# Other orders of rounding, turns, sums and loads at ten places of a two-block fp32 kernel

## The reference

```python
# block 1, layer 0: the input is a norm of x, scaled and shifted by rows of c @ w_mod + b_mod
u = h @ w_in                         # q, k, v, gates, z for 4 heads of 256; the pool's input
y_m = head_norm(mlstm(q, k, v) + mlstm_reversed(q, k, v)) * sigmoid(...) * silu(...)
y_p = ((window_mean(u) - u) @ pool_w) * scale * silu(...)     # windows 2, 4, 8, 16
x = x + gate * norm(concat(y_m, y_p) @ w_out)
# block 1, layer 1: 16 heads of 64 over 4 key heads, rotary positions, window of 128 and context, a sink
x = x + gate * norm((attention(q, k, v) * silu(z)) @ w_out)
# block 2
x = x + concat(gla(...), diff_attention(...)) @ w_out         # 4 heads each
x = x + (silu(conv(h @ w_up_a)) * conv(h @ w_up_b)) @ w_down  # 2816 wide
x = x + sigmoid(h @ w_gate) * (p @ w_proj)                    # the "ple" stage
out = norm(x) * norm_final
```

## Time and profile before

| | us |
|---|---|
| median of 3 runs | 3405.12 (3401.29 to 3410.22) |
| the profiled execution's own time | 3408.22 |
| its span in the trace | 3406.4 |
| PE busy | 3296.8 (17536 products) |
| DVE busy | 1765.3 |
| ACT busy | 1510.5 |
| POOL busy | 110.6 |
| mean granted clock of PE | 0.988 |

### The profile page before, as it was taken

How to read it: one execution, slowest core, us unless ns; L and a number is a source line. 1 busy time by engine, 2 the same in 40 slices (tenths; PEclk the granted TensorE clock), 3 DMA queues, 4 the chain that set the end, 5 groups by cost and what they waited for, 6 DMA issues and landing times. The chain is left out here.

```text
span 3406.4 us, 42773 instructions
## 1 busy us (share of the span) xinstructions
PE 3296.8 (97%) x17536; PEld 2664.9 (78%) x17536; DVE 1765.3 (52%) x2736; ACT 1510.5 (44%) x2411; POOL 110.6 (3%) x240
## 2 busy tenths in 40 slices
PE   7999999999999999999999999998999999999997
PEld 5988889797777777887887777775778888878775
DVE  6544444444344467532886644359556544444544
ACT  5343434434224345215786534228435444433445
POOL 2000000000000000001000000000000000000000
PEclk8999999999999999999999999999999999999999
DMA  5202011111333556122301711010331111134553
GB/s 203 70 1 81 29 54 55 53 56 38 141 134 105 190 207 247 56 50 71 91 2 38 195 53 50 26 54 1 130 118 50 50 50 43 44 130 161 179 185 130
DMA packets 187442, 308.38 MB, mean 91 GB/s; under 512 B 28507, under 2 KB 122560, under 8 KB 187120
## 3 DMA queue, kind: packets, MB, share of 16 engines
q1 hardware_dynamic: 165392, 227.60, 20.8%
q0 software_dynamic: 20784, 77.98, 6.5%
q10 hardware_dynamic: 1072, 0.07, 0.0%
HBM read 269.87 MB, written 35.75 MB: 90 GB/s over the span
## 5 line engine op out<-in xcount | busy, mean ns | idle before, releaser
L412 DVE TENSOR_TENSOR W_rounded<-W,W_rounded 128x2048 fp32r<-128x2048 f32 (+1 forms) x172 | 348.9, 2029 | 469.5 <-ACT W_rounded L403 465.7
L403 ACT ACTIVATE W_rounded<-W 128x2048 fp32r<-128x2048 f32 (+1 forms) x172 | 292.5, 1701 | 398.2 <-DMA W<-in_w_down 97.0
L3587 PE MATMUL G<-HT_rounded,W_rounded 128*128 128x512 f32 x1584 | 452.8, 393 | 0.0
L3587 PEld LDWEIGHTS G<-HT_rounded,W_rounded 128*128 128x128 f32 x1584 | 298.3, 188 | 68.4
L2551 PE MATMUL G<-W_rounded,r_y_rounded 128*128 128x512 f32 x960 | 229.7, 400 | 6.1 <-DVE r_y_rounded L2657 4.7
L2551 PE MATMUL G<-W_rounded,x_hi 128*128 128x512 f32 x704 | 222.1, 397 | 3.6 <-DVE act_turned_rounded L2657 3.3
L2551 PEld LDWEIGHTS G<-W_rounded,r_y_rounded 128*128 128x128 f32 x960 | 181.0, 190 | 51.7 <-DVE W_rounded L412 5.7
L2204 PE MATMUL G<-HT_rounded,W_rounded 128*128 128x512 f32 (+1 forms) x768 | 210.1, 358 | 3.7 <-DVE W_rounded L412 3.7
L1151 PE MATMUL G<-W_rounded,HT_rounded 128*128 128x512 f32 x640 | 213.6, 415 | 0.0
L3587 PE MATMUL G<-HT_lo_ffn,W_rounded 128*128 128x512 f32 x528 | 208.5, 395 | 0.0
L1195 PE MATMUL G<-HT_rounded,W_rounded 128*128 128x512 f32 (+1 forms) x768 | 205.7, 354 | 1.0 <-PEq L652 1.0
(11 more groups left out here) (479 smaller groups left out, 6468.9 us busy)
## 6 DMA issues: line engine op xcount, KB each, us to landing
W<-in_w_down SPq DMA_DIRECT2D x33, 1024.0 KB, 4.9
W<-in_ab_w_out SPq DMA_DIRECT2D x32, 1024.0 KB, 5.5
W<-in_w_up SPq DMA_DIRECT2D x44, 512.0 KB, 5.0
W<-in_ab_w_in SPq DMA_DIRECT2D x20, 1024.0 KB, 8.7
W<-in_w_mod SPq DMA_DIRECT2D x8, 2048.0 KB, 8.1
x_rows<-r_xt POOLq DMA_DIRECT2D x32, 512.0 KB, 5.5
W<-in_c_w_out SPq DMA_DIRECT2D x24, 512.0 KB, 7.0
r_xt<-x_rows POOLq DMA_DIRECT2D x24, 512.0 KB, 5.1
```

The source lines that it names most:

```text
L403: ins = a.activation(self.half(key, True)[:, at], self.half(key, False, False)[:, at], ACT.Copy)
L412: ins = v.tensor_tensor(self.half(key, False)[:, at], self.half(key, False, False)[:, at], self.half(key, True)[:, at].bitcast(F32), ALU.s ...
L3587: ins = pe.matmul(bank(("up", j, half))[:, rc * 512:rc * 512 + 512], w[a][:, k, c], x[b][:, 2 * rc:2 * rc + 2, :], start=(k == 0 and a == ...
```

## The change

Ten places get another order; no weight product is added or removed.

1. Start: one 1 MB load moves from SP's queue to POOL's; DVE copies the fourth part's rows ahead of two low parts, and rounds the first weight half after them.
2. Heads: the rounding of the next head's first half is done in four pieces at steps 11 to 14 instead of one at step 10.
3. The four late turns are made in two pairs, after the first and second row chunk of the first gemm, and ACT's copies with them; the same at the seam to the pool.
4. Pool: `wlo(1)` comes before `prev.done(v)` and the windows.
5. Attention: the last block's rounding is split into head pairs 0 to 6 and pair 7.
6. `rows_part`, gated: `before_split(s)` row sums come before the rounding, the others after it. Not gated: all row sums come before the following stage's rounding.
7. `rows_part`, `tail`: the up projection's first piece is rounded at the end of the step instead of before the row work.
8. Differential attention: the small loads move from SP to POOL, the scores of steps 2 to 15 alternate between the halves of `S`, GLA's turns go to the upper half of `TP` with one buffer instead of two, and one instruction gets another form.
9. ple: the gates of the last two rows follow their Relu; the last projection goes into a free bank of G.
10. ple: the last row's product, sum, scaling and store are made in halves, and stored by SP.

```diff
@@ phase_start
-            for j in range(4):
+            for j in (0, 2, 3):
                 load_mod(sp, j, 0)
...
-            for j in range(4):
+            load_mod(g, 0, 1)
+            for half in range(2):
+                load_mod(g, 1, half)
+            for j in (2, 3):
                 load_mod(g, j, 1)
...
             mod_rows(2)
+            mod_rows(3)
             low(2)
-            mod_rows(3)
             mod_cols(2)
-            low(3)
             mod_cols(3)
             shifts(4)
             value(4)
             value(6)
+            for k in range(3, KT):
+                low(k)
             K.split_lo(v, ("qk", 0, 0))
-            for k in range(4, KT):
-                low(k)
@@ mlstm_part: tensor, (scalar alike), vector
-                if ct == 0 and h >= 1:
-                    for n in late:
-                        turn_y(pe, h - 1, n)
+                    if h >= 1 and ct == 0 and rc < 2:
+                        for n in late[2 * rc:2 * rc + 2]:
+                            turn_y(pe, h - 1, n)
...
-                if s == 10:
-                    K.split_lo(v, ("qk", h + 1, 0) if h + 1 < H else ("p", 0, 0))
+                if 11 <= s < 15:
+                    K.split_lo(v, ("qk", h + 1, 0) if h + 1 < H else ("p", 0, 0), s - 11, 4)
@@ attend_part
+    rounded = [(bi, 0, 8) for bi in range(XT - 1)] + [(XT - 1, 0, 7), (XT - 1, 7, 8)]
@@ pool_part: tensor, vector
+                if (gi, ct) == (0, 0) and rc_ < 2:
+                    prev.turn(pe, rc_)
...
                 if gi == ct == 0:
+                    wlo(1)
                     prev.done(v)
...
-                if gi == ct == 0:
-                    wlo(1)
@@ rows_part: scalar and vector
+    def before_split(s):
+        rows = ended(s)
+        if per >= 8:
+            return 1
+        return len(groups[s // per]) if s < len(steps) else len(rows)
...
-            for r in rows[:1] if per >= 8 else rows:
+            for r in rows[:before_split(s)]:
                 act_y(r)
...
-            if s == len(steps) and following:
+            if not gated:
+                for r in ended(s):
+                    add(r)
+            if s == len(steps) + int(not gated) and following:
                 K.split_lo(v, following[1])
...
-            for r in ended(s)[:1] if per >= 8 else ended(s):
-                add(r)
+            if gated:
+                for r in ended(s)[:before_split(s)]:
+                    add(r)
...
-                if tail is not None:
-                    tail[2](v, 0)
...
                     B.vec_turned(v, r, TR, *turned(r))
+            if s == len(steps) - 1 and tail is not None:
+                tail[2](v, 0)
@@ diff_part
-    gla_steps = [1, 3, 5, 7, 9, 11, 13, 14]
+    gla_steps = [1, 3, 5, 7, 9, 11, 13, 15]
...
+    def s_at(j):
+        return 512 * ((j + 1) % 2) if 2 <= j < 16 else 0
...
-            if j >= 1:
+            if j == 2:
+                mix.taken(pe)
+            elif 3 <= j < 16:
+                pe.wait_ge(s_nm, 2 * j - 2)
+            elif j >= 1:
                 pe.wait_ge(s_nm, 2 * j)
...
-            if r >= 2:
-                pe.wait_ge(s_gl, r - 1)
+            if r >= 1:
+                pe.wait_ge(s_gl, r)
...
-            if j == 16:
+            if j == 18:
                 pe.wait_ge(s_gl, XT)
...
-            ch.link(v.tensor_scalar(cw[:, j:j + 1], sm[:, j, 0:1], rc[:, j, 1:2], lam[:, 3:4], ALU.mult, ALU.mult))
+            ch.link(v.scalar_tensor_tensor(out=cw[:, j:j + 1], in0=sm[:, j, 0:1], scalar=lam[:, 3:4], in1=rc[:, j, 1:2],
+                                           op0=ALU.mult, op1=ALU.mult))
@@ ple_part
+    def product(r):
+        return G[:, (r + 1) % 3, :] if r == XT - 1 else PP[:, :]
...
-            if r:
+            if r == XT - 1:
+                pe.wait_ge(s_gread, r - 1)
+            elif r:
                 pe.wait_ge(s_pp, r)
...
+                    if s == len(steps):
+                        gate(r)
...
+                halves = [slice(0, 512), slice(512, D)] if r == XT - 1 else [slice(0, D)]
...
-            for r in due(s, 2):
+            for r in [] if s == len(steps) else [XT - 3, XT - 2] if s == len(steps) + 2 else due(s, 2):
```

More of the change, by code:

```diff
@@ L1269, in evacuate @@
                 K.free_bank(a.activation(raw[:, ct % 2, p0:p0 + n], G[:, K.par(key), 0:n], ACT.Copy), key)
+                if h >= 1 and ct == 0 and rc < 2:
+                    for q in late[2 * rc:2 * rc + 2]:
+                        copy_turned_y(a, h - 1, q)
         def take_v(h, r):
@@ L2602, in scalar @@
                     a.activation(y_part(s, 1), y_part(s, 0, False), ACT.Copy).then_inc(s_yhi, 1)
-            if s == len(steps) - 1:
-                if following:
-                    K.split_hi(a, following[0])
-                if tail is not None:
-                    tail[1](a, 0)
-            for r in rows[1:] if per >= 8 else []:
+            if s == len(steps) - 1 and following:
+                K.split_hi(a, following[0])
+            for r in rows[before_split(s):]:
                 act_y(r)
@@ L2658, in vector @@
                         .then_inc(s_ylo, 1)
-            if s == len(steps) - 1:
-                if following:
-                    K.split_lo(v, following[0])
-                if tail is not None:
-                    tail[2](v, 0)
-            for r in ended(s)[1:] if per >= 8 else []:
+            if s == len(steps) - 1 and following:
+                K.split_lo(v, following[0])
+            for r in ended(s)[before_split(s):] if gated else []:
                 add(r)
@@ L3250, in sync @@
     def sync(sp):
[L3251 to L3256 removed]
+        pass
     def turn_diff(pe, bi):
@@ L3826, in scalar, with gate @@
         ch = Chain(a, K.a_chain, K.an)
+        def gate(r):
+            e = ge[:, r % 3, :]
+            a.wait_ge(s_gread, r + 1)
+            ch.link(a.activation(e, e, ACT.Exp, bias=K.cut[:, :], scale=-1.0))
+            ch.link(a.activation(e, e, ACT.Ln, bias=K.one[:, :]))
+            a.activation(e, e, ACT.Exp, scale=-1.0).then_inc(s_sg, 1)
         for s in range(2, len(steps) + 5):
```

108 lines of the change are left out of this document (56 added, 52 removed).

## The result

The changed kernel takes 3369.7 us (median of 4 runs, 3365.7 to 3374.2) against 3406.9 us (median of 4, 3401.3 to 3410.2): 37.1 us less, a ratio of 0.9883 with a 95% interval of 0.9864 to 0.9903. The forecast was 39.1 us less and 3366.

A forecast was written before the change was run, and what follows sets the result against it. PE was taken to bound the kernel, busy 3296.8 of 3406.4 us, leaving 109.6 us idle and half-clock stretches to win. Ten terms summed to 39.1 us off the 3405.1 median: 3366, range 3352 to 3388.

The forecast's parts named there:

- three signs of being wrong: PE idle time falling under 20 us, new waits over 1 us where a rounding moved, PE busy time moving over 10.
- Start: At the start, DVE's earlier copy removes a 1.63 us wait and the moved load gives 0.7: −2.3 us (0 to −5).
- the rule weighed in the forecast: Transfers from any engine share 16 DMA engines; the start's moved load would give 0 instead of 0.7, forecast 3366.7.
- Heads: In four heads, quartered rounding removes four 1.59 us waits, −6.4; late turns in pairs give 0.8 each, −3.2.
- Pool: At the pool, DVE's earlier rounding removes PE's 3.67 us wait and 3.0 of half clock: −6.7 us (−3.7 to −6.8).
- End of attention, out2, down, end: Four terms: attention's split rounding −1.0, out2 to up −1.5, down −2.4, program end −5.6 us, 3.9 from the projection's room.
- out1: the step that failed: In out1, two sums before the rounding save 2.5 of 2.64 us, plus 1.5 of clock: −4.0 (−2.5 to −4.2).
- The late third sum delays one row's norm by 2.3 us, which has no reader on PE near: In out1, moving the third row sum behind the rounding was claimed to delay nothing that PE soon needs.
- Differential attention: Early small loads −1.7, banks −1.1 and −0.7, new instruction form 2.5 counted of 3.7: −6.0 us (−3 to −10).
- Half of it: Rival: gaps at every seam move to the next wait instead of going; 20 us gained, 3385 us; chance 0.23.
- More clock: Rival: half-clock stretches behind seams at 48, 1857, 2290, 2311, 2516 also go, about 2 us each: 3356; chance 0.12.
- Slower by the quarters: Rival: in the heads, 16 rounding quarters behind the state update each cost PE a wait; chance of slower 0.02.

The follow-up runs named there:

- out1_sums_back: The changed kernel with all three row sums of an out1 group again ahead of the next weight half's rounding; 3380.5 us, ratio 0.9916 to the kernel before.

## Why the prediction was right, point by point

**Size and sign.** The forecast of 39.1 us met 37.1, inside its range and beyond what a measurement can tell from no change. It did so with two terms much too large and several too small, which is luck in part: out1 and differential attention were forecast at 10.0 and gave 0.8 in the pair of traces.

**The forecast's own signs.** It named three signs of being wrong, and two of them came. PE's idle time fell by 26.2 us, more than the 20 that it asked for. But a new wait of 2.8 us stands in out1, with a stretch of 3.4 us at 0.50 behind it where the forecast wanted 1.00, and PE's busy time moved by 16.3 us, more than 10: some 16 of the 42.5 us between the two traces are the clock, and the forecast's sum had about 6 for it. So the total is right, and the account behind it only in part. DVE's busy time fell by 0.3 us and not by 3.7: the new form saved 1.8 (8.8 to 7.0), and the 16 quarters cost 1.8 more than the four roundings (11.0 against 9.2).

**Start.** The wait of 1.63 us and part of those for the loads went as said. The size was off: −5.6 in the pair, −3.7 by the middle of 11 executions, against −2.3. Part of the rest is the clock, 10.2 us at 0.50 in the profiled execution and 17.1 before, which the forecast had in its upper bound. By the rule weighed in the forecast the moved load would have given 0, and by itself it did (67.3 against 67.2). DVE's order with the old loads brought 0.3. The forecast took the two for a sum, and only together do they give anything that is seen.

**Heads.** The mechanism was right: all four waits for the state update are gone, and no quarter (685 ns, as forecast) brought one of them back. The terms were undersized: 1.8 instead of 1.59 for a rounding, 1.0 instead of 0.8 for a block.

**Pool.** The sum was right enough (−9.3, forecast −7.5), the reason was half of it. The forecast gave the whole wait of 3.67 to DVE's moved rounding; the turns in pairs, which it had priced at 0.8, would have taken most of it alone through the store and the table. The stretch at the lower clock went with the wait, as said. Of the 9.3 us, 1.7 are a second stretch at 0.50 near the stage's end (3.4 us from 1116.3), which the forecast did not have and which two later kernels have again (284.5 us instead of 282.8).

**End of attention, out2, down, end.** −1.2, −1.5, and −5.5 against −1.0, −1.5, and −5.6. Down with the following gemm gave −4.3 against −2.4, of which down's stretch of 3.4 us at 0.50 is part: it is there before and in none of the later kernels, though the wait of 1.9 us at its place stays. That all of these come from the edits named is argued from the waits that went, since no kernel undoes them. At the end of the program the time was right and the weights of the causes weren't: the forecast put 3.9 of 5.6 on the room of the projection, and it is the gates and the room together.

**out1: the step that failed** is "The late third sum delays one row's norm by 2.3 us, which has no reader on PE near". It has: DVE's row work of the same step is behind the sum, ACT's high part of the row behind that, ACT's and DVE's rounding of the next half behind that, and PE waits there for 2.8 us. Forecast −4.0, in the pair +0.4, and −1.5 to −2.2 against the changed kernel with the sum behind the row work too, since the row is then wanted in the next stage.

**Differential attention: the term that was mis-sized.** Of −6.0, −1.2 came in the pair, −0.7 by the middle of eight executions. PE's idle time in the stage did fall, from 18.7 to 15.9 us, but the steps are a ring of ACT's exponentials, DVE's share and weighing, PE's turn and ACT's copy, with ACT's norm in it every fourth step. What one place gave was waited for at the next, and part of the idle time came back at the lower clock: both traces have 10.2 us at 0.50 in the stage, of which PE was busy for 8.2 before and for all after. The form of the small instruction was priced by a row whose scalar is a constant in the instruction, where here it is read from a tile: 53 ns gained, not 115. That this operand is the reason is not shown.

**What the forecast did not have:** −1.7 in up and the more than 1 us in down. In up this is the clock: the gap of 3.16 us some 9 us into the stage is 2.84, and the stretch at 0.50 there is 3.4 us or none in all the later kernels instead of 6.8. What shortened it is not shown.

**The rivals.** Half of it: this is what out1 and differential attention did; the whole did not, since heads, pool and end kept their gains. More clock: happened in part, 16.3 us of PE's busy time, where the forecast's terms held about 6 (3.0, 1.5 and 1.5 at the end). Of the five stretches that this rival named, the one at 48 is gone and the one at 2516 is half as long; the one behind the seam and the 10.2 us of differential attention are still there. Slower by the quarters: no.

## What to carry to other kernels

Before a wait is booked as gain, follow the instruction that was moved behind it: which engine's next high part, copy or load stands behind, and when PE wants that. A gain stays where one engine had idle time ahead of the wait (heads, pool) and moves where three engines follow each other in a ring. When two edits end near one wait, undo each and both: each alone can look worth nothing (0.9 and 1.1 of 5.8 us; 0.9 and 3.1 of 6.5 us). When a stage's time scatters, sort its executions by how long the clock was low in it before an edit is priced.

## What the runs showed of the hardware

While PE had work, its stretches at a granted clock of 0.50 lasted 3.4, 6.8 or, in four traces, 10.2 us, 34 to 58 us in all in the traces of the changed kernel and its variants and 71.7 before. Most stand behind a gap of PE of 1 us or more, but not behind each such gap: in the same stage, behind a gap of 2.8 us, one execution has such a stretch and the next has none (up: 492.2 us with none, 493.4 to 493.7 with 3.4 us of it, 495.1 before with 6.8). In differential attention, with the same order, they go with 116.2 to 118.9 us. So a single execution's total can't tell an edit of a microsecond or two.

A stage that streams weights and rows has its own scatter: out0, whose order no kernel here changes, took 239.7 to 248.7 us. In out1 a load of 1 MB landed 5.3 us after its issue in the trace before and 8.2 us in that of `out1_sums_back`, which has the same order there.
